# Attention's four projections as 2x2 block products with seven half products, in a hybrid decoder step

## The chip, the cores and the metric

The kernel runs on one core of one Trainium2 chip, as one program in one launch. The metric is the device time in microseconds. Profiles are of one execution each.

## The reference, cut to what matters

```python
D_MODEL, SEQ, DEC_BATCH, PAST_LEN, PAGE_SIZE = 1024, 1024, 8, 1024, 128
B_HEADS, B_DH = 16, 64
def trunk(x, ...):                       # prompt: 1 x 1024 rows; samples: 8 rows with a paged cache
    h, s = hgrn_layer(x, ...)            # first half: gated linear recurrence, 8 heads
    u = rms_norm(h, norm_kv)
    k, v = split(u @ w_kv)               # 1024 x 1024 each
    k = rms_norm(k per head, k_norm)
    logf = log_sigmoid(u @ w_fgate + b_fgate)
    q, gate = split(rms_norm(h, norm_g) @ w_in)    # 1024 x 1024 each
    q = rms_norm(q per head, q_norm)
    # causal for the prompt; for a sample: 1024 cached keys and its own
    p = softmax(q k^T / 8 + c_q - c_k)   # c: cumulative logf, per head
    o = (p @ v) * silu(gate)
    return h + o @ w_o
```

All data is float32. The prompt's 1024 rows and the 8 samples are treated as N = 1032 columns of one matrix `h_t` (features on the partitions).

## The kernel before

The program is written engine by engine with semaphores; each engine runs its own list in the order in which it is written out, and a wait holds up everything behind it on that engine. There are three stages: the recurrence over eight heads (to about 655 us), its output projection with the norm over nine tiles of rows (`tile`, to about 809 us), and the attention, which this change is about.

The attention runs over PAIRS = 8 pairs of heads, `pair(p)` in each engine's list. Each pair has 128 columns of the four projections k, q, v and gate (here g). On TensorE a projection is three pieces of 344 columns by eight blocks of 128 features (`kq`, `values`, `gate_in`), written into banks 0 and 1 in turn; the order of these and of the small products (means of squares for the norms, transposes of k, of v and of the samples) is one list, `ring_order`, and ScalarE empties every one of them (`kq_out`, `v_out`, `g_out`, and so on).

The prompt's attention goes in eight rows of 128 queries: `scores(p, i)` on TensorE, `row_max(p, i)` on VectorE, `soft(p, i)` on ScalarE (exponential, sum, normalised weights), `turn_rows(p, i)` on TensorE (transposes), copies by `turn_a` (ScalarE) and `turn_v` (VectorE), and every second row the product with the values, `weighted(p, m)`. From row 4 on a row fills all four banks of scores, so its `scores` wait for the row before to be turned and copied. Between these steps TensorE does pieces of the projections of this pair (v, g) and of the next (k, q).

The samples' attention over the cache: SyncE loads blocks of 512 KB of cached keys into a ring of four (`k_in`) and of cached values (`v_in`); GpSimd multiplies each block with the queries (`times_q`, line 720); VectorE reduces it (`score`, line 1500); `tops` on VectorE forms the maxima and on GpSimd reduces them over the partitions (line 702), after which come `shift`, `dec_e`, `weigh`, TensorE's `decode`, `smp_sum`, `turn_num` and `smp_out`. Two groups of four samples a pair, both within the pair. The queries of the samples go to memory and come back spread over the partitions (`q_spread`, lines 707 to 710).

The gate: `gate_abs`, `gate_ln`, `gate_in`, `gate_sig` and `gate` for pair p run in pair p + 1. The outputs of all heads stay in `o_t`. VectorE also scales each loaded weight block by the norm's gain (`scale_w`, line 392). At the end `y_part` multiplies all heads' outputs by w_o.

The first half of the kernel already has the scheme that the change brings to the attention. `unit` (line 1694) is one of fourteen units, each of four matmuls of 258 columns, for two projections at once; `unit_copy` (ScalarE) empties two of seven units and `unit_add` (VectorE, line 1149) adds the other five; `w_sums` (GpSimd, lines 627 to 630) forms the sums of weights.

In the trace one float32 matmul of the program is two instructions.

## Time and profile before

| | us |
|---|---|
| time, median of 3 runs (lowest, highest) | 1737.03 (1736.64, 1741.09) |
| the profiled execution | 1736.7 |
| its span, first to last instruction | 1735.0 |
| the recurrence | 0 to 655 |
| output projection and norms | 655 to 809 |
| start of the attention | 809 to 859 |
| pairs 0 to 6 | 859 to 1524, about 95.5 each |
| pair 7 and the output projection | 1524 to 1735 |

The mean granted clock of TensorE is 0.988 of its full rate. A reader of such a profile looks at the busy times of the engines first, then at the same table by stretches, then at what each wait of the busiest engine was for, and last at the other engines in order of time, since an engine's list can be late although its busy share is low.

### The profile page before, as it was taken

The page shows a single profiled execution, that of the slowest core. Times are in us where ns is not written, and L with a number is a line of the kernel's source. Part 1 is how long each engine was busy: PE and PEld are TensorE (multiplying, and loading weights), DVE is VectorE, ACT ScalarE, POOL GpSimd, SP SyncE. Part 2 cuts the span into 40 slices and gives each one's busy share as a digit, 9 for nine tenths or more (in the row PEclk, how much of TensorE's full clock was granted, in tenths as well). Part 3 has the DMA queues.
Part 4 walks back from the last instruction along what each step waited for, and adds up shares of the span by engine and source line. Part 5 has one row for each costly group of instructions (what it writes and reads, how often), then busy time and mean ns, then how long its engine had stood idle before and what let it go on. Part 6 is the DMA issues. An engine that isn't in the chain of part 4 may idle for free.

```text
span 1735.0 us, 23215 instructions
## 1 busy us (share of the span) xinstructions
PE 1666.4 (96%) x8777; PEld 1156.8 (67%) x8777; DVE 966.1 (56%) x1746; ACT 665.4 (38%) x1296; POOL 374.5 (22%) x273
## 2 busy tenths in 40 slices
PE   6999999999999999999999999999999999998998
PEld 4787878888888886443566666666666666665443
DVE  6668695868677775212345546455465655464310
ACT  3324242333323242111345454455454454544100
POOL 5022232222222200100140323222140412232000
PEclk9999999999999999999999999999999999999999
DMA  9480927365463723423324435243525444272121
GB/s 259 143 257 26 267 63 219 96 186 146 135 184 104 233 90 111 129 87 115 90 74 140 164 110 194 99 158 110 171 85 159 134 137 167 86 245 96 49 83 40
DMA packets 252226, 235.94 MB, mean 136 GB/s; under 512 B 22843, under 2 KB 219643, under 8 KB 252115
## 3 DMA queue, kind: packets, MB, share of 16 engines
q1 hardware_dynamic: 241970, 201.04, 37.8%
q0 software_dynamic: 10144, 33.42, 5.7%
q8 instruction: 70, 1.15, 0.3%
q14 instruction: 42, 0.34, 0.1%
HBM read 209.46 MB, written 92.07 MB: 174 GB/s over the span
## 4 chain that ended last, share of the span: by engine, by line
PE 82%; DVE 7%; ACT 4%; issue 4%; DMA 2%; POOL 1%; SPq 0%; DVEq 0%; ACTq 0%; POOLq 0%
PE psum L1694 18%; PE psum L1890 13%; PE psum L1701 7%; PE psum L2106 6%; PE psum L1754 6%; PE psum L1929 5%; PE psum L1954 4%; PE psum L1906 4%; PE psum L1975 3%; PE psum L1961 3%; PE psum L1669 2%; PE psum L1996 2%; PE psum L1898 1%; PE psum L1792 1%; DVE arena L1245 1%
## 5 line engine op out<-in xcount | busy, mean ns | idle before, releaser
L1694 PE MATMUL psum<-arena 128*128 128x258 f32 x1680 | 400.0, 391 | 20.5 <-DVE arena L1149 12.9
L1694 PEld LDWEIGHTS psum<-arena 128*128 128x128 f32 x1680 | 316.3, 194 | 80.6 <-DVE arena L1149 18.7
L1890 PE MATMUL psum<-arena 128*128 128x344 f32 x768 | 236.9, 459 | 1.4 <-DVE arena L1354 0.7
L1890 PEld LDWEIGHTS psum<-arena 128*128 128x128 f32 x768 | 141.9, 191 | 81.6 <-issue 8.4
L720 POOL TENSOR_TENSOR arena<-arena 128x1024 f32<-128x1024 f32 x64 | 160.2, 2532 | 116.6 <-issue 113.2
L976 ACT ACTIVATE arena<-psum,arena 128x256 f32<-128x256 f32 (+7 forms) x128 | 93.6, 737 | 162.1 <-DVE arena L1436 162.1
L1149 DVE TENSOR_TENSOR arena<-arena,psum 128x258 f32<-128x258 f32 x150 | 62.8, 419 | 129.3 <-PE psum L1694 128.8
L1444 DVE COPY arena<-psum 128x128 f32<-128x128 f32 (+3 forms) x64 | 48.4, 756 | 151.6 <-PE psum L1961 151.2
L2106 PE MATMUL psum<-arena 128*128 128x512 f32 (+1 forms) x288 | 127.2, 600 | 2.9 <-DVE arena L1484 2.9
L1701 PE MATMUL psum<-arena 128*128 128x512 f32 (+1 forms) x288 | 128.0, 600 | 0.1
L1929 PE MATMUL psum<-arena 128*128 128x344 f32 x384 | 118.9, 464 | 0.0
L1906 PE MATMUL psum<-arena 128*128 128x344 f32 x384 | 117.9, 457 | 0.0
L1754 PEld LDWEIGHTS psum<-arena 128*128 128x128 f32 x896 | 108.1, 192 | 4.5 <-issue 1.0
L1754 PE MATMUL psum<-arena 128*128 128x64 f32 x896 | 106.1, 271 | 0.0
L2106 PEld LDWEIGHTS psum<-arena 128*128 128x128 f32 (+1 forms) x288 | 51.4, 181 | 73.9 <-issue 70.7
L1929 PEld LDWEIGHTS psum<-arena 128*128 128x128 f32 x384 | 71.9, 192 | 39.9 <-issue 6.8
L1906 PEld LDWEIGHTS psum<-arena 128*128 128x128 f32 x384 | 71.8, 192 | 37.6 <-ACT arena L922 2.0
L1701 PEld LDWEIGHTS psum<-arena 128*128 128x128 f32 (+1 forms) x288 | 51.1, 181 | 68.6 <-issue 68.6
L985 ACT ACTIVATE arena<-arena 128x256 f32<-128x256 f32 (+7 forms) x128 | 92.4, 769 | 2.1
L822 ACT ACTIVATE arena<-arena 128x1024 f32<-128x1024 f32 x56 | 59.2, 1058 | 84.5 <-DVE arena L1188 83.4
L1954 PE MATMUL psum<-arena 64*128 64x512 f32 (+3 forms) x384 | 79.5, 518 | 8.6 <-DVE arena L1444 8.6
L1500 DVE TENSOR_REDUCE arena<-arena 128x16 f32<-128x1024 f32 x64 | 76.4, 1215 | 17.7 <-POOL arena L720 17.4
(246 smaller groups left out, 2364.7 us busy)
## 6 DMA issues: line engine op xcount, KB each, us to landing
k_pages<-in_cache_k SPq DMA_DIRECT2D x64, 512.0 KB, 6.5
v_pages<-in_cache_v SPq DMA_DIRECT2D x64, 512.0 KB, 7.0
arena<-k_pages SPq DMA_DIRECT2D x64, 512.0 KB, 4.0
arena<-v_pages SPq DMA_DIRECT2D x64, 512.0 KB, 5.4
arena<-in_w_in_a SPq DMA_DIRECT2D x32, 512.0 KB, 6.9
arena<-in_x_prompt SPq DMA_DIRECT2D x16, 512.0 KB, 6.2
arena<-in_w_kv SPq DMA_DIRECT2D x16, 512.0 KB, 5.5
arena<-in_w_in_b SPq DMA_DIRECT2D x16, 512.0 KB, 6.3
```

Of the source, the lines that this page charges most:

```text
L720: pool.tensor_tensor(k_ring[:, b], k_ring[:, b], q_all[:, HALF * g + b:HALF * g + b + 1, :].broadcast_to([P, PAGES, P]), ALU.mult).then_in ...
L976: ins = act.activation(weights[:, x, 0:n], rows[:, x, 0:n], ACT.Exp, bias=top[:, at:at + 1], scale=-1.0, accum_out=total[:, at:at + 1])
L985: act.activation(weights[:, x, 0:n], weights[:, x, 0:n], ACT.Copy, scale=inv[:, at:at + 1]).then_inc(p_set, 1)
L1500: dve.tensor_reduce(lg[:, b, :, 0:PAGES].rearrange("p x j -> p j x"), k_ring[:, b].rearrange("p j (x d) -> p j x d", x=2), AX.X, ALU.add). ...
L1694: ins = pe.matmul(bank[n % 2][:, 0:PIECE], w[:, k, :], x[:, k, :], start=(k == 0 and r in (0, 1, 3, 4)), stop=(k == HK - 1), skip_group_ch ...
L1701: ins = pe.matmul(dst[0:rows, :], o_heads[h][:, cols(t)], w_o[:, h, 512 * j:512 * j + 512], start=(h == 0 or lo == AH - 1), stop=(h == AH ...
L1754: ins = pe.matmul(bank[2 + l % 2][:, t * UPPER:(t + 1) * UPPER], f[:, t * P:(t + 1) * P], q, start=True, stop=True)
L1890: ins = pe.matmul(slot[name][:, 0:W3], (w_k, w_q)[y][:, k, :], h_t[:, k, part3(n)], start=(k == 0), stop=(k == KT - 1))
L1906: ins = pe.matmul(slot[f"g{n}"][:, 0:W3], w_g[:, k, :], h_t[:, k, part3(n)], start=(k == 0), stop=(k == KT - 1))
L1929: ins = pe.matmul(slot[f"v{n}"][:, 0:W3], w_v[:, k, :], h_t[:, k, part3(n)], start=(k == 0), stop=(k == KT - 1))
L1954: ins = pe.matmul(dst[:, x, lo:hi], q_t[p % 2][rows, cols(i)], k_t[p % 2][rows, lo:hi], start=True, stop=True)
L2106: ins = pe.matmul(bank[j][0:rows], o_t[:, h, cols(t)], w_ob[h][:, 512 * j:512 * j + 512], start=(h == 0), stop=(h == AH - 1))
```

## The change

The four projections become two pairs of projections (k with q, v with g), each a 2x2 block product: the 1024 features are two halves, the 1032 columns are two halves, and with sums of the inputs (`x_sum`, formed once) and sums of the weights (formed for each pair) seven half products do the work of eight. A pair of projections is fourteen units, each four matmuls of 252 or 264 columns. ScalarE copies two of seven units and VectorE adds the other five.

Around it: `ring_order` becomes `item_order`, since the small products now go through bank 7 alone. The sums of squares for the norms are taken from k_t and q_t in memory (`squares`) and no longer from PSUM. SyncE's ring of cached keys is two blocks, not four. The samples of pair p are decoded in rows that reach into pair p + 1, one reduction to a row. The gate of pair p is done in pair p. Heads' outputs of pairs 0 to 5 are stored to memory (`o_store_b`) and loaded again before the output projection. The input sums overwrite parts of `o_t` and of `h_t`, and the start of the attention is rearranged around them. The first half is as it was, but for its units being 252 and 264 columns.

```diff
-PIECE = HN // 2
+SPLIT = (0, 252, HN)
@@ GpSimd
+            def block_sums(one, two, out, done):
+                me.did(pool.tensor_tensor(out[:, 0], two[:, 0:HK], two[:, HK:KT], ALU.add))
+                me.chain(pool.tensor_tensor(two[:, 0:HK], one[:, 0:HK], two[:, 0:HK], ALU.subtract))
+                me.chain(pool.tensor_tensor(out[:, 1], out[:, 0], one[:, 0:HK], ALU.subtract))
+                pool.tensor_tensor(out[:, 2], one[:, HK:KT], out[:, 1], ALU.subtract).then_inc(done, 1)
+            def sums_of_kq(q):
+                pool.wait_ge(w_k_scaled, q + 1)
+                pool.wait_ge(w_q_scaled, q + 1)
...
             def pair(p):
-                pool.wait_ge(q_loaded, 16 * (p + 1))
-                times_q(p, 0)
-                pool.wait_ge(ring.taken, ring.at("vt1", p))
-                pool.dma_start(v_out[:, :, p, :], v_cur).then_inc(v_stored, 16)
+                m = S * p
+                if p:
+                    times_q(m - 3)
+                if p + 1 < PAIRS:
+                    sums_of_kq(p + 1)
+                k_store(p)
+                q_out(p)
+                if p:
+                    times_q(m - 2, m - 1)
+                q_in(p)
+                if p:
+                    tops(p - 1, 1)
+                v_store(p)
+                times_q(m, m + 1)
+                if p + 1 < PAIRS:
+                    sums_of_vg(p + 1)
+                times_q(m + 2, m + 3)
                 tops(p, 0)
...
+                if 0 < p <= OWN:
+                    o_store_b(p - 1)
+                times_q(m + 4)
@@ VectorE, pair p, from row 0
                 row_max(p, 0)
                 if p:
+                    fin(p - 1, 3)
+                    weigh(p - 1, 0)
+                    score(m - 3)
                 turn_v(p, 0)
+                vg_add(p, 10)
+                if nxt:
+                    scale_w(dve, w_q, gain_b, p + 1, w_q_loaded, w_q_scaled)
                 row_max(p, 1)
+                if p:
+                    smp_sum(p - 1, 0)
+                vg_add(p, 11)
+                vg_add(p, 12)
+                if p:
+                    score(m - 2)
                 turn_v(p, 1)
+                vg_add(p, 13)
+                gate_abs(p)
                 row_max(p, 2)
...
                 row_max(p, 3)
+                kq(3)
+                if p:
+                    shift(p - 1, 1)
+                gate_in(p)
+                kq(4)
                 fin(p, 0)
+                score(m)
                 turn_v(p, 3)
+                kq(5)
                 row_max(p, 4)
...
+                kq(6)
+                silu(p)
+                score(m + 1)
                 if nxt:
                     scale_w(dve, w_v, gain_kv, p + 1, w_v_loaded, w_v_scaled)
+                turn_v(p, 4)
+                kq(8)
                 row_max(p, 5)
...
+                if nxt:
+                    scale_w(dve, w_g, gain_b, p + 1, w_g_loaded, w_g_scaled)
+                kq(11)
+                score(m + 2)
+                turn_v(p, 5)
...
+                turn_v(p, 7)
                 if nxt:
                     norm(p + 1, 0)
+                vg(8)
                 if p + 2 < PAIRS:
                     scale_w(dve, w_k, gain_kv, p + 2, w_k_loaded, w_k_scaled)
                 if nxt:
                     norm(p + 1, 1)
@@ ScalarE, pair p
                 soft(p, 3)
+                if p:
+                    dec_e(p - 1, 1)
+                gate_ln(p)
                 turn_a(p, 3)
+                new_in(p)
                 soft(p, 4)
+                kq(7)
+                gate_sig(p)
                 turn_a(p, 4)
+                kq(9)
                 soft(p, 5)
@@ TensorE, pair p
                 scores(p, 0)
                 if p:
                     weighted(p - 1, 3)
+                vg(p, 9)
+                turn_k(p, 0)
+                if p:
+                    decode(p - 1, 0)
+                turn_rows(p, 0)
+                vg(p, 10)
+                turn_k(p, 1)
+                turn_smp(p)
                 scores(p, 1)
+                vg(p, 11, 12)
...
                 turn_rows(p, 1)
+                vg(p, 13)
                 scores(p, 2)
+                kq_n(0)
+                turn_values(p, 0)
+                kq_n(1)
...
                 scores(p, 3)
+                kq_n(3)
+                weighted(p, 0)
+                kq_n(4)
                 turn_rows(p, 3)
+                new_score(p)
+                kq_n(5)
                 scores(p, 4)
```

## Rows read from the trace of the kernel before

**Rows 1.** The page's first part: busy us, share of the span and instructions of each engine.

```profile
PE 1666.4 (96%) x8777; PEld 1156.8 (67%) x8777; DVE 966.1 (56%) x1746; ACT 665.4 (38%) x1296; POOL 374.5 (22%) x273
```

**Rows 2.** Table by stretches: busy of PE, PEld, DVE, ACT, POOL, then granted clock, DMA.

```profile
1146.00:1241.00 95.00, 93.59 (x559) 60.90 (x557) 51.79 (x116) 49.47 (x111) 25.00 (x16) 1.00 0.43 139
```

**Rows 3.** TensorE's waits in the stretch of one pair, 1146 to 1241.5.

```profile
PE psum L1954 <- DVE arena L1444: 1.0, 1, 1.0
```

**Rows 4.** GpSimd in order of time over one pair: start, duration, instruction, idle before.

```profile
1171.77 1.08 POOL L727 DMA_DIRECT2D out_v_prompt<-arena  x1 [4.17 <-ACT arena L966]
1179.84 0.40 POOL L702 PARTITION_ALL_REDUCE arena<-arena  x1 [6.99 <-issue]
1180.11 0.73 POOL L730 DMA_DIRECT2D out_v_sample<-arena  x1
1187.70 10.29 POOL L720 TENSOR_TENSOR arena<-arena 128x1024 f32<-128x1024 f32 x4 [6.87 <-issue]
1237.07 0.73 POOL L707 DMA_DIRECT2D out_k_sample<-arena  x1 [0.47 <-ACT arena L941]
1237.81 0.52 POOL L708 DMA_DIRECT2D q_rows<-arena  x1
1244.62 0.59 POOL L710 DMA_DIRECT2D arena<-q_rows  x1 [6.29 <-DMA q_rows<-arena]
```

**Rows 5.** The page's groups of instructions: the projections before (busy us, mean ns).

```profile
L1890 PE MATMUL psum<-arena 128*128 128x344 f32 x768 | 236.9, 459 | 1.4 <-DVE arena L1354 0.7
L1929 PE MATMUL psum<-arena 128*128 128x344 f32 x384 | 118.9, 464 | 0.0
L1906 PE MATMUL psum<-arena 128*128 128x344 f32 x384 | 117.9, 457 | 0.0
```

**Rows 6.** The chain that ended last: sixteen instructions of 344, and of 258 columns.

```profile
1164.45 4.84 PE psum L1890 x16
...
72.30 3.54 PE psum L1694 x16
```

**Rows 7.** Groups of VectorE: addition of a unit, reduction of a block, scaling of weights.

```profile
L1149 DVE TENSOR_TENSOR arena<-arena,psum 128x258 f32<-128x258 f32 x150 | 62.8, 419 | 129.3 <-PE psum L1694 128.8
L1500 DVE TENSOR_REDUCE arena<-arena 128x16 f32<-128x1024 f32 x64 | 76.4, 1215 | 17.7 <-POOL arena L720 17.4
L392 DVE TENSOR_TENSOR arena<-arena 128x1024 f32<-128x1024 f32 x32 | 46.3, 1449 | 8.8 <-DMA arena<-in_w_kv 8.6
```

**Rows 8.** GpSimd in order of time: a weight sum while VectorE is quiet.

```profile
38.00 1.27 POOL L629 TENSOR_TENSOR arena<-arena 128x512 f32<-128x512 f32 x1
```

**Rows 9.** Groups of GpSimd: the four weight sums, over the first half.

```profile
L629 POOL TENSOR_TENSOR arena<-arena 128x512 f32<-128x512 f32 x15 | 41.6, 2772 | 1.2
L630 POOL TENSOR_TENSOR arena<-arena 128x512 f32<-128x512 f32 x15 | 38.2, 2549 | 1.2
L628 POOL TENSOR_TENSOR arena<-arena 128x512 f32<-128x512 f32 x15 | 24.9, 1659 | 0.0
L627 POOL TENSOR_TENSOR arena<-arena 128x512 f32<-128x512 f32 x15 | 20.4, 1359 | 159.0 <-PE psum L1694 156.5 <-DMA arena<-in_w_in_a 2.5
```

**Rows 10.** TensorE, then ScalarE, in order of time: row 3, weighted(p, 3), the gate.

```profile
1171.24 1.13 PE L1954 MATMUL psum<-arena 64*128 64x512 f32 x4
1237.76 3.46 PE L1975 MATMUL psum<-arena 128*64 128x256 f32 x32
...
1175.95 1.34 ACT L985 ACTIVATE arena<-arena 128x512 f32<-128x512 f32 x2
1240.87 1.05 ACT L1002 ACTIVATE arena<-arena 128x1032 f32<-128x1032 f32 x1
```

**Rows 11.** TensorE in order of time: a decode in a pair, and after a wait.

```profile
1200.94 1.93 PE L1996 MATMUL psum<-arena 128*2 128x128 f32 x64
...
1580.12 0.39 PE L1991 MATMUL psum<-arena 128*128 128x8 f32 x2 [2.50 <-DVE arena L1522]
1580.44 3.57 PE L1996 MATMUL psum<-arena 128*2 128x128 f32 x64
```

More of the change, by code:

```diff
@@ L744, in _ @@
+            times_q(S * PAIRS - 1)
+            tops(PAIRS - 1, 1)
+            for t in range(2, TT + 1):
                 pool.wait_ge(yb_v, 2 * t + 2)
@@ new lines, in sm_out, with vt_out @@
+            def sm_out(q):
+                act.wait_ge(items.done, items.at("sm", q))
+                if q:
+                    act.wait_ge(ks_stored, 16 * q)
+                    act.wait_ge(q_stored, 16 * q)
+                act.copy(smp_tok[0:S], bank[7][0:S, 0:2 * P]).then_inc(items.taken, 1)
+            def vt_out(p, j):
+                act.wait_ge(items.done, items.at(f"vt{j}", p))
+                if j == 0 and p:
+                    act.wait_ge(pv_done, 4 * p)
+                    act.wait_ge(v_stored, 16 * p)
+                act.copy(v_cur[:, 4 * j:4 * j + 4, :], bank[7]).then_inc(items.taken, 1)
@@ new lines, in new_in @@
+            def new_in(p):
+                act.wait_ge(items.done, items.at("sn", p))
+                if p:
+                    act.wait_ge(df_set, 2 * p)
+                for g in range(2):
+                    lg = lgt[g].rearrange("p (b x j) -> p b x j", x=2, j=9)
+                    ins = act.activation(lg[:, :, :, PAGES], bank[7][:, 8 * g:8 * g + 8].rearrange("p (b x) -> p b x", x=2), ACT.Copy,
+                                         scale=-float(P))
+                ins.then_inc(items.taken, 1)
@@ L1894, in means, with open_item @@
[L1894 to L1908 removed]
+            def open_item(name, p):
+                n = items.next(name, p)
+                if n > 1:
+                    pe.wait_ge(items.taken, n - 1)
+                return bank[7]
@@ new lines, in b_unit @@
+            def b_unit(n, one, two, w_sum, scaled, summed, u):
+                if u == 0:
+                    for s in scaled:
+                        pe.wait_ge(*s)
+                elif u == 1:
+                    pe.wait_ge(*summed)
+                if n in (1, 4, 8, 11):
+                    pe.wait_ge(h_sums, {1: 3, 4: 7, 8: 7, 11: 8}[n])
+                if n >= 2:
+                    pe.wait_ge(*b_units.taken(n - 2))
+                product(n, one[:, 0:HK], one[:, HK:KT], two[:, 0:HK], two[:, HK:KT], w_sum, u).then_inc(b_units.done, 1)
@@ new lines, in kq, with vg, means @@
+            def kq(q, *us):
+                for u in us:
+                    b_unit(kq_b(q, u), w_k, w_q, sums_kq, ((w_k_scaled, q + 1), (w_q_scaled, q + 1)), (kq_sums, q + 1), u)
+            def vg(p, *us):
+                for u in us:
+                    b_unit(vg_b(p, u), w_v, w_g, sums_vgb, ((w_v_scaled, p + 1), (w_g_scaled, p + 1)), (vgb_sums, p + 1), u)
+            def means(q, y, *ns):
+                for n in ns:
+                    dst = open_item(f"m{'kq'[y]}{n}", q)
+                    pe.wait_ge(sq_done, 2 * q + y + 1)
+                    pe.matmul(dst[:, 0:W3], bones, sq[y][:, part3(n)], start=True, stop=True, skip_group_check=True).then_inc(items.done, 1)
```

1091 lines of the change are left out of this document (572 added, 519 removed).

## The prediction

> **What bounds the kernel now.** I read the page's engine table first: TensorE is busy for 1666.4 us of a 1735.0 us span and GpSimd for 374.5 us [rows 1]. A reader should ask next whether TensorE's work is really end to end, so the second view is the table by stretches. The attention repeats every 95.5 us, once for each of eight pairs of heads. In one such stretch of 95 us TensorE is busy for 93.6 us, VectorE for 51.8, ScalarE for 49.5 and GpSimd's recorded instructions for 25.0 [rows 2]. Its only wait of note in a pair is that of the first scores, 1.0 us, for a VectorE copy [rows 3]. So today the attention is bound by TensorE, and an operation less on it is time won as long as the other engines keep ahead. The third view, GpSimd in order of time, shows that its busy share is misleading: around each of the two partition reductions of a pair it does nothing on record for 6.9 to 7.0 us, once before it and once after it, marked "issue", though no operand is late [rows 4]. Four such gaps a pair are 28 us, so GpSimd is really taken for 25 + 28 = 53 of 95 us.
>
> **What is removed.** The four projections of a pair are 192 instructions of 344 columns, 1536 in all [rows 5]. Sixteen of them take 4.84 us in the chain, and 0.19 us of that is the tail of the group, so one costs 0.289 us; sixteen of 258 columns, the form that the first half of the kernel already uses, take 3.54 us, 0.2165 us each with the tail out [rows 6]. A pair goes from 192 x 0.289 = 55.5 us to 28 units x 8 x 0.2165 = 48.5 us. That is 7.0 us a pair and 56 us in all, the most the change can give. TensorE's own work for a pair becomes 93.6 - 7.0 = 86.6 us; the walk below, operation by operation, comes to 86.
>
> **What is added.** VectorE gets 20 additions from PSUM a pair at 0.42 us [rows 7], 8.4 us, and loses about 0.5 us of gating, so about 60 of 87 us. ScalarE loses some 3 us. GpSimd gets two sets of four weight sums. Their cost has two ends: 1.27 us each when nothing else reads, 5.1 us a set [rows 8], and the means 1.36, 1.66, 2.77 and 2.55 us of the first half, 8.3 us a set [rows 9]. I take 6 us, near the lower end, because in the attention VectorE mostly reads PSUM while they run, and keep both ends. GpSimd then has 53 + 12 (10 to 17) us, and about 8 us more of waiting for the trip of the queries through memory, since it now waits for it explicitly: 73 us of a pair. It fits on paper. What decides is order, since VectorE takes its work strictly in turn and several items in its list wait for GpSimd.
>
> **The order, walked through for one middle pair.** Times are from the pair's first scores; durations are those of the rows, and copies and maxima that have no row of their own are taken as in the same operation before. VectorE scales w_q after row 0, at 12.3 (TensorE's part before it is the 3.4 us product of row 7, two units, the 2.0 us decode [rows 10, 11] and short transposes). GpSimd can only then form the k/q sums (to 18.3). It next issues the stores of keys and queries (2.4 us, two of their rows in [rows 4]) and then multiplies cached block m-2, 2.5 us, to 23.2. But VectorE has the reduction of that block, 1.2 us [rows 7], ahead of turning row 1, which TensorE has ready at 16.4. So turn_v(1) ends at 24.8 instead of 16.8, the last value unit is added at 25.2, and unit kq 1, which needs its bank, waits on TensorE from 21.7 to 25.3. Row 2's maximum is queued behind too, and the first head's weights come about 3.5 us after that maximum begins (in row 3, a size larger, they come 4.3 us after the end of the scores, at 1176.6 for scores that end at 1172.3 [rows 10]). Scores of row 3 end at 35.9 instead of 28.0: loss 7.9 us.
>
> Second, in row 3 VectorE must run the gate's second step before turn_v(3), and that step waits for two ScalarE passes of 1.05 us [rows 10] which sit behind row 3's softmax: ready at 44.2, then an addition, a copy and the reduction of block m. GpSimd has m only at 47.2 (18.3, stores 2.4, two multiplications 5, waiting for the queries' store and fetching them 1.9, a gap of 7.2, the reduction 0.9, stores of values 1.8, a gap of 7.2, a multiplication 2.5). TensorE ran out of work at 42.9 and gets row 3 back at 49.2: loss 6.3, of which 4.0 would be there without GpSimd.
>
> Third, in row 4 VectorE's silu waits for ScalarE's sigmoid, which waits for the copy of unit kq 7, and turn_v(4) is behind silu (1.2), a reduction (1.2) and a weight scaling of 1.2 to 2.5 us (1.45 on average [rows 7]). TensorE has only row 4's transposes and one unit meanwhile: loss 3.9 with a small wait before the decode. Fourth, row 5 has the reduction of block m+2 ahead of turn_v(5), and GpSimd makes the v/g sums, which wait for w_g scaled in that same row, ahead of that block: 6 + 2.5 us after the scaling. Loss 5.5. Fifth, at the pair's end the norm of q, which the next pair's first scores need, is queued on VectorE behind the addition of unit vg 8 (that waits for a ScalarE copy) and a scaling of w_k; with row 7 that is 3.9 us. Small waits make 0.3.
>
> Sum: 7.9 + 6.3 + 3.9 + 5.5 + 3.9 + 0.3 = 27.8 us of waiting over about 86 us of work, a pair of 113.8 us against 95.5: 18.3 us more. Every step from turn_v to turn_v is a loop through all engines, so none of it is made up in the next pair.
>
> **The clock.** After TensorE idled 2.50 us late in the kernel, the 64 instructions of a decode took 3.57 us where they take 1.93 us in a pair without such a wait [rows 11]. That is the step between the levels 2.4 and 1.2 GHz. With five or six idle stretches of 2 to 6 us a pair, some of whose slow work lies where TensorE waits anyway, I add 4 us a pair (0 to 9, from 1.6 us times none or all of them). The granted clock should fall from 1.00 in a pair to about 0.9.
>
> **The ends.** The stretch between the first half and the pairs takes over 23 units (39.8 us against 27.8 of projections) and eight input subtractions of about 1.2 us on VectorE, half of them under earlier tiles: 8 us later at pair 0. Pair 0 has no block of a pair before it in rows 1 and 2: 4.5 us longer than now. The last pair has five units instead of 48 instructions of each projection it had (19 us less work), but the same waits in rows 2 to 6 with GpSimd's gaps: 6 us less in all. The extra stores and loads of the heads' outputs (about half a megabyte each) run on queues that wait for little; I cost them at nothing beyond GpSimd's issue time, as the product that needs them comes one pair later; if that cover were gone, some 5 us once.
>
> Sum against the profiled execution, 1736.7 us (1.7 of it outside the span, and 0.3 below the median of the runs): 1736.7 + 8 + 4.5 + 6 x 18.3 - 6 + 7 x 4 = 1881, so **1880 us**.
>
> **A rule beside the rows.** The gaps of [rows 4] have no instruction in the trace. The Trainium skill's GPSIMD Engine Reference, Instruction dispatch, says that the first call of a freshly loaded kernel pays a load of approximately 6 us with no visible instruction. The trace agrees in kind, with 6.9 to 7.0 us. By 6 us in place of 7.2 the chain to row 3 would be 2.4 us shorter, of which 2.2 count before VectorE's own order binds, 13 us in all: 1868. The same page, Key points, says that GpSimd contends with VectorE instructions with two SBUF inputs; it speaks against the change, as the third rival does from rows.
>
> **Rivals.**
> *Everything is hidden and TensorE stays the bound.* For it: 93.6 of 95 us busy, and the same units with the same sums run in the first half with few waits. Against it: there, no reduction of a block waits behind the sums, and no reduction gap either. It would give 7.0 a pair back, less a little: 1736.7 - 56 + 5 = 1685. It is the case with the other sign; it decides if turn_v(1), (3) and (5) are done before TensorE has finished the unit after them. Chance 0.12.
> *GpSimd is early, but the order on VectorE and ScalarE holds.* Then row 1 loses nothing, row 3 loses 4.0, row 4 3.9, row 5 0, the end 3.9, a pair is about 98.6 + 2 for the clock: 5.1 x 6, and 8, 2 and -7 at the ends, 1770. It needs the sums and gaps to be half of what the rows show, or the scaled weights some 10 us earlier. Chance 0.2.
> *The upper prices.* Sums of 8.3 us twice, gaps of 8.2 us and all the slow clock: 4.6 + 2 + 5 more a pair, 1881 + 6 x 11.6 = 1950. Chance 0.08.
> Forecast 0.58. The change not doing what it says (a projection left whole) has 0.02; the instruction counts would show it, and the time would be near the old.
>
> **From cases to numbers.** The range goes from 1765, to take in the second rival, to 1935: the forecast's own is 1830 to 1930 (clock 0 to 9 a pair). That leaves out 0.12 + 0.02 below and about half of the upper prices. Faster by over 0.3% 0.12, within 0.3% 0.02, slower by more 0.86; 0.3% is about what a measurement of this kernel can tell from no change.
>
> **What would show it.** Right: a pair of 108 to 124 us; GpSimd or a reduction of a cached block named as what VectorE waited for before turn_v(1), (3), (5); 20 to 30 us of idle TensorE a pair; four gaps of about 7 us a pair still there; a lower granted clock. Wrong: TensorE over 97% busy in a pair of 88 us (first rival), or VectorE reductions that never wait for GpSimd with a pair near 100 us (second). The forecast fails first if the sums take under 4 us or if VectorE reaches the scaling of w_q much earlier than 12 us into the pair.

## The result and the profile after

The changed kernel takes 1921.42 us (median of 4 runs, 1920.36 to 1924.78) against 1739.06 us (1736.64 to 1741.81) for the kernel before on the same chip: a ratio of 1.105, 95% interval 1.103 to 1.108. The forecast was 1880 us, with a range of 1765 to 1935. The profiled execution spans 1918.7 us, 183.7 more than before.

First the page's engine table of the changed kernel, to hold against [rows 1], and then its table by stretches for pair 3, to hold against [rows 2] (busy time of PE, PEld, DVE, ACT, POOL, granted clock, DMA share, GB/s).

```profile
PE 1698.4 (89%) x9033; PEld 1241.1 (65%) x9033; DVE 1024.4 (53%) x1911; ACT 646.2 (34%) x1248; POOL 454.2 (24%) x343
```

```profile
1222.00:1344.50 122.50, 100.52 (x593) 72.49 (x593) 58.87 (x137) 47.59 (x104) 35.47 (x25) 0.89 0.33 112
```

The change takes matmul columns away, and yet TensorE is busy for longer, 100.5 us of a pair for 93.6. The clock in the same row says why it isn't more work: 0.89 for 1.00. And 22.0 us of the pair are idle where there was 1.4. These are TensorE's four largest kinds of wait in that pair (total, times, longest), where [rows 3] had one of 1.0 us:

```profile
PE psum L2126 <- DVE arena L1576: 11.9, 3, 4.4
PE psum L2126 <- DVE arena L1534: 3.0, 1, 3.0
PE psum L2133 <- ACT arena L1068: 2.8, 2, 2.3
PE psum L1861 <- DVE arena L1230: 2.2, 1, 2.2
```

L2126 are the scores and L1576 is turn_v, the copy of the turned weights out of PSUM: the scores of rows 4, 5 and 6 wait for it. The others are the next pair's first scores behind the norm of q (L1534), `turn_rows` (L2133) behind ScalarE's weights, and unit kq 1 (L1861) behind the addition that frees its bank (L1230). VectorE's own waits in that pair tell what held the copy back. L1636 is the reduction of a cached block (`score`), L1604 is silu, L1600 the gate's second step:

```profile
DVE arena L1636 <- POOL arena L790: 12.1, 2, 7.0
...
DVE arena L1604 <- ACT arena L1084: 5.4, 1, 5.4
...
DVE arena L1600 <- ACT arena L1080: 4.3, 1, 4.3
```

GpSimd in order of time in that pair (start, duration, idle before) answers to [rows 4]:

```profile
1235.80 1.27 POOL L658 TENSOR_TENSOR arena<-arena 128x512 f32<-128x512 f32 x1 [23.87 <-issue]
...
1239.73 1.28 POOL L661 TENSOR_TENSOR arena<-arena 128x512 f32<-128x512 f32 x1
1240.95 1.08 POOL L774 DMA_DIRECT2D out_k_prompt<-arena  x1
...
1243.14 4.67 POOL L790 TENSOR_TENSOR arena<-arena 128x1024 f32<-128x1024 f32 x2
...
1255.80 0.39 POOL L757 PARTITION_ALL_REDUCE arena<-arena  x1 [6.81 <-issue]
...
1265.92 5.65 POOL L790 TENSOR_TENSOR arena<-arena 128x1024 f32<-128x1024 f32 x2 [8.19 <-issue]
```

The reader sees the first loss whole: weight sums, stores, and only at 1243.14 the product of block m-2. The 23.87 us of "issue" ahead of the sums are a wait too: they begin as soon as VectorE has scaled w_q (L418, first line below), and the second set, at 1298.84, as soon as it has scaled w_g (last line). So GpSimd's lateness itself comes out of VectorE's list. On VectorE the reduction of m-2 stands ahead of turn_v(1):

```profile
1234.45 1.22 DVE L418 TENSOR_TENSOR arena<-arena 128x1024 f32<-128x1024 f32 x1
...
1245.55 1.22 DVE L1636 TENSOR_REDUCE arena<-arena 128x16 f32<-128x1024 f32 x1 [5.13 <-POOL arena L790]
1246.68 0.41 DVE L1576 COPY arena<-psum 128x256 f32<-128x256 f32 x1
...
1267.07 2.29 DVE L1600 SCALAR_TENSOR_TENSOR arena<-arena 128x1032 f32<-128x1032 f32 x1 [4.27 <-ACT arena L1080]
...
1269.95 1.21 DVE L1636 TENSOR_REDUCE arena<-arena 128x16 f32<-128x1024 f32 x1
1271.07 0.68 DVE L1576 COPY arena<-psum 128x512 f32<-128x512 f32 x1
...
1297.48 1.22 DVE L418 TENSOR_TENSOR arena<-arena 128x1024 f32<-128x1024 f32 x1
```

Last, what follows the idle stretches on TensorE in the same pair:

```profile
1290.07 2.57 PE L2126 MATMUL psum<-arena 64*128 64x512 f32 x8 [3.25 <-DVE arena L1576]
...
1308.59 3.36 PE L2126 MATMUL psum<-arena 64*128 64x512 f32 x8 [4.38 <-DVE arena L1576]
1311.88 3.81 PE L2149 MATMUL psum<-arena 128*64 128x256 f32 x24
```

The first scores of the pairs start at 871.30, 979.12, 1100.09, 1221.93, 1344.45, 1465.35, 1587.10 and 1708.46. So of the 183.7 us, 11.9 arise before pair 0 (which began at 859.45), 16.3 in pair 0, 156.3 in pairs 1 to 6 (26.1 each, a pair being 121.6 for 95.5), and 0.8 come back at the end.

### The profile page after: what moved, and what is told of

It is laid out like the page before. It is cut to its first block and busy times, and to the rows that moved or that the text cites. A ratio compares the mean times of both kernels' runs of the same rounds, so it can differ in the third digit from the quotient of the medians.

```text
span 1918.7 us, 24200 instructions
## 1 busy us (share of the span) xinstructions
PE 1698.4 (89%) x9033; PEld 1241.1 (65%) x9033; DVE 1024.4 (53%) x1911; ACT 646.2 (34%) x1248; POOL 454.2 (24%) x343
## 5 line engine op out<-in xcount | busy, mean ns | idle before, releaser
L1861 PE MATMUL psum<-arena 128*128 128x252 f32 (+1 forms) x3472 | 854.3, 398 | 36.5 <-DVE arena L1230 28.2
L1861 PEld LDWEIGHTS psum<-arena 128*128 128x128 f32 x3472 | 666.8, 198 | 182.9 <-issue 53.1
L1230 DVE TENSOR_TENSOR arena<-arena,psum 128x252 f32<-128x252 f32 (+1 forms) x310 | 129.8, 419 | 269.3 <-PE psum L1861 254.7
L2126 PE MATMUL psum<-arena 64*128 64x512 f32 (+3 forms) x384 | 108.3, 681 | 114.4 <-DVE arena L1576 95.0
L790 POOL TENSOR_TENSOR arena<-arena 128x1024 f32<-128x1024 f32 x64 | 153.8, 2419 | 148.5 <-issue 97.0
L658 POOL TENSOR_TENSOR arena<-arena 128x512 f32<-128x512 f32 x31 | 40.4, 1305 | 540.2 <-issue 336.4
L1059 ACT ACTIVATE arena<-psum,arena 128x256 f32<-128x256 f32 (+7 forms) x128 | 93.6, 737 | 220.8 <-DVE arena L1568 220.8
L2126 PEld LDWEIGHTS psum<-arena 64*128 64x128 f32 x384 | 44.3, 243 | 162.6 <-issue 138.9
L868 ACT COPY arena<-psum 128x252 f32<-128x252 f32 (+1 forms) x124 | 45.8, 369 | 299.1 <-PE psum L1861 299.1
L1636 DVE TENSOR_REDUCE arena<-arena 128x16 f32<-128x1024 f32 x64 | 77.8, 1216 | 93.3 <-POOL arena L790 93.0
L1938 PEld LDWEIGHTS psum<-arena 128*128 128x128 f32 x896 | 108.2, 192 | 4.4 <-issue 1.0
L2133 PE MATMUL psum<-arena 128*128 128x128 f32 x576 | 81.1, 281 | 22.8 <-ACT arena L1068 22.4
L2133 PEld LDWEIGHTS psum<-arena 128*128 128x128 f32 x576 | 63.9, 142 | 45.7 <-ACT arena L1068 39.6
L2149 PE MATMUL psum<-arena 128*64 128x256 f32 (+1 forms) x640 | 88.2, 434 | 0.0
L1576 DVE COPY arena<-psum 128x128 f32<-128x128 f32 (+3 forms) x64 | 48.1, 752 | 64.3 <-PE psum L2133 64.2
```

Source lines behind the costliest of these rows:

```text
L790: pool.tensor_tensor(k_ring[:, m % 2], k_ring[:, m % 2], q_all[:, m % S:m % S + 1, :].broadcast_to([P, PAGES, P]), ALU.mult).then_inc(kq_m ...
L1059: ins = act.activation(weights[:, x, 0:n], rows[:, x, 0:n], ACT.Exp, bias=top[:, at:at + 1], scale=-1.0, accum_out=total[:, at:at + 1])
L1230: dve.tensor_tensor(out, more, bank[n % 2][:, 0:size(u)], ALU.add).then_inc(of.by_dve, 1)
L1636: dve.tensor_reduce(lg[:, b, :, 0:PAGES].rearrange("p x j -> p j x"), k_ring[:, m % 2].rearrange("p j (x d) -> p j x d", x=2), AX.X, ALU.a ...
L1861: ins = pe.matmul(bank[n % 2][:, 0:size(u)], w[:, k, :], x[:, k, :], start=(k == 0 and r in (0, 1, 3, 4)), stop=(k == HK - 1), skip_group_ ...
L1938: ins = pe.matmul(bank[2 + l % 2][:, t * UPPER:(t + 1) * UPPER], f[:, t * P:(t + 1) * P], q, start=True, stop=True)
```

## Experiments

**First set: each of the four causes alone.** Four kernels, each one edit of the changed kernel. The first moves every reduction of a cached block behind the turn_v that it stood ahead of (row 1 shown, rows 2 to 5 alike):

```diff
@@ VectorE, pair p
-                if p:
-                    score(m - 2)
                 turn_v(p, 1)
                 vg_add(p, 13)
                 gate_abs(p)
                 row_max(p, 2)
+                if p:
+                    score(m - 2)
```

> Only VectorE's list is changed: in rows 1 to 5 the reduction of a cached block stands behind the row's turn_v, not ahead of it. Theory (order: TensorE waits because turn_v(1) and turn_v(5) are queued behind blocks that GpSimd has late): TensorE no longer waits 2.2 + 2.3 us in row 2 and 4.4 us ahead of the scores of row 6, but shift(p-1,1) in row 3 then waits for GpSimd's partition reduction for some 4 us. A pair goes from 121.6 to about 108 us, the time from 1921 to about 1830 (ratio to before 1.05). Rival (the cost is the gaps and the work of GpSimd itself, which stays): no change, a pair of 120 us. Rival (the cost is the unit scheme and the slow clock): no change either.

Measured: 1856.61 us, ratio 1.067 (1.065 to 1.069), 65 us less than the changed kernel; a middle pair 112.6 us, pair 0 94.0. The direction is the theory's, the size isn't (about 1830 and 108 us): with the blocks out of the way gate_abs came to lie beside GpSimd's products and took 5.60 us for 0.91, and TensorE waited 4.74 us ahead of turn_rows(2). The kernel with all edits of order, below, shows the same in its rows.

The second moves the next pair's norm of q, with its new score, ahead of the last unit and the scaling of w_k:

```diff
-                vg(8)
-                if p + 2 < PAIRS:
-                    scale_w(dve, w_k, gain_kv, p + 2, w_k_loaded, w_k_scaled)
                 if nxt:
                     norm(p + 1, 1)
                     new_score(p + 1)
+                vg(8)
+                if p + 2 < PAIRS:
+                    scale_w(dve, w_k, gain_kv, p + 2, w_k_loaded, w_k_scaled)
```

> Only the end of a pair on VectorE is changed: the norm of the next queries and new_score stand ahead of the addition of unit 8 and of the scaling of w_k. Theory (order): the 2.9 us that TensorE waits before the first scores of each pair goes, 3 us in each of seven pairs, 21 us, ratio to before about 1.093. Rival (ScalarE's norm steps are what is late): no change.

Measured: 1887.83 us, ratio 1.084 (1.082 to 1.087), 34 us less, with no wait left ahead of the first scores. That is more than the 21 us expected: the product behind these scores, weighted(p - 1, 3), takes 3.46 us for 5.02, so the slower work behind the wait went with it.

The third leaves out the maximum over the partitions, and so GpSimd's four gaps a pair; the decode then subtracts another value:

```diff
-                pool.partition_all_reduce(m_all[g], top8[g], P, bass.bass_isa.ReduceOp.max).then_inc(top_all, 1)
+                pool.tensor_copy(m_all[g], top8[g]).then_inc(top_all, 1)
```

> The maximum over the partitions in the samples' softmax is left out: GpSimd copies the partition's own maxima. With it all four code loads of a pair go, some 28 us of GpSimd's time. Theory (order): GpSimd has block m ready about 1 us before VectorE asks for it, and waits for VectorE at both weight sums, so the gaps are not on the path: a pair within 1.5 us of 121.6, ratio to before 1.09 to 1.105. Rival (GpSimd's gaps are the cost): up to 14 us a pair less, 90 us in all, ratio 1.05.

Measured: 1897.04 us, ratio 1.090 (1.088 to 1.093), 24 us less, just inside the theory's range of ratios. A middle pair is 118.7 us for 121.6, 2.8 less where the theory had at most 1.5, though some 28 us of gaps left GpSimd in it; another 8.1 us came back in the last part. VectorE still waits 12.0 us a pair for the products of blocks m-2 and m+2, which stand behind the weight sums.

The fourth moves the gate's second step from ahead of kq 4 to behind row_max(4), and silu from ahead of turn_v(4) to behind row_max(5):

```diff
-                gate_in(p)
                 kq(4)
...
                 row_max(p, 4)
+                gate_in(p)
...
-                silu(p)
...
                 row_max(p, 5)
+                silu(p)
                 gate_first(p)
```

> Only the gate's places on VectorE are changed: gate_in goes from ahead of turn_v(3) to behind the maximum of row 4, silu from ahead of turn_v(4) to behind the maximum of row 5. Theory (order): the waits of 4.3 and 3.3 us ahead of the scores of rows 4 and 5 shrink to about 0 to 1, block m then being what row 3 waits for, about 6 us a pair and 1 to 2 more by the clock, 50 us in all, ratio to before about 1.075. Rival (GpSimd late in row 3): row 3 gains nothing and the whole less than 25 us.

Measured: 1879.96 us, ratio 1.081 (1.079 to 1.083), 41 us less, for the 50 expected. VectorE's waits for GpSimd in a pair rose from 12.1 to 16.4 us at once: with the gate out of the way, block m is what holds row 3. There the rival was right, since TensorE's wait ahead of the scores of row 4 went only from 4.25 to 3.93 us; the gain is row 4's own, where the wait of 3.25 us ahead of the scores of row 5 is gone.

**Is it the weight sums or GpSimd's other lateness?** Here three of four operations of each set are left out in pairs 1 to 7 (so q, k, v and the gate come out as other values):

```diff
+            def last_sum(one, two, out, done):
+                pool.tensor_tensor(out[:, 2], one[:, HK:KT], out[:, 1], ALU.subtract).then_inc(done, 1)
...
-                block_sums(w_k, w_q, sums_kq, kq_sums)
+                (block_sums if q == 0 else last_sum)(w_k, w_q, sums_kq, kq_sums)
```

> Left out: the first three of the four operations of each set of weight sums of attention's pairs 1 to 7 on GpSimd (the last one stays, so the stages keep their signals; the outputs are not the reference's). That takes 3.8 of 5.1 us a set off GpSimd, twice a pair. Theory (the sums stand ahead of the decode blocks on GpSimd, and VectorE takes each block ahead of a turn_v): block m-2 is ready 3.8 us sooner in row 1 and block m+2 sooner by up to 7.0 us, the wait that VectorE had for it, of which 3.8 go: 7.6 us a pair at most, and TensorE's time after the waits shortens with its clock: 50 to 70 us in all, 1850 to 1872 us, ratio 1.065 to 1.077. Rival (GpSimd's lateness is that of its waits for VectorE and DMA, or VectorE's own queue binds right behind): under 20 us, 1901 to 1920, ratio above 1.094.

Measured: 1849.90 us, ratio 1.064 (1.062 to 1.066), 72 us less for 3.8 us off each set. VectorE still waits for GpSimd, and for the gate as before:

```profile
DVE arena L1639 <- POOL arena L793: 6.7, 3, 3.1
DVE arena L1607 <- ACT arena L1087: 5.4, 1, 5.4
```

So the sums are a cause of their own. A set stands before a block that stands before a turn_v, and 7.6 us of GpSimd's time became about 11 of the pair (110.4 for 121.6 on average). In pair 3, 110.1 us for 122.5, TensorE idles for 16.1 us instead of 22.0 and is busy for 93.9 instead of 100.5, so about half of the gain is the clock. The wait ahead of the scores of row 6 fell from 4.38 to 0.48 us, while that ahead of row 4, which is the gate's, grew from 4.25 to 5.64.

**Is the slow work after a wait really the wait's doing?** Two kernels add work to TensorE where it idles, ahead of the scores of rows 4, 5 and 6: multiplications of the identity by itself, 24, 18 and 24 of them in the first.

```diff
+                def fill(u, count):
+                    n = kq_b(p + 1, u)
+                    if nxt:
+                        pe.wait_ge(*b_units.taken(n - 2))
+                        for _ in range(count):
+                            pe.matmul(bank[n % 2][:, 0:128], ident, ident, start=True, stop=True, skip_group_check=True)
...
                 last((1, 0, 3))
+                fill(6, 24)
...
                 last((1, 3, 5))
+                fill(9, 18)
...
-                kq_n(12, 13)
+                kq_n(12)
+                fill(13, 24)
+                kq_n(13)
```

> The changed kernel with work added: 24, 18 and 24 matmuls of 128x128 with the identity, whose output nobody reads, on TensorE where it idles ahead of the scores of rows 4, 5 and 6 of every pair but the last. At the full clock one is about 0.13 us (0.130 for a transpose of that size), so 3.1, 2.3 and 3.1 us in idle stretches of 4.25, 3.25 and 4.38 us; nothing that TensorE waits for moves. Theory (idle stretches cost their length and then again at the lower clock that is granted after them; 8.6 us of a pair were put down to that): the scores of rows 4 to 6 come back to their full-clock 2.0 to 2.3 us from 2.5 to 3.4, weighted(2) to 2.6 from 3.8, the granted clock rises from 0.943 to 0.96 or more, and the kernel is faster by 2 to 6 us a pair: 1880 to 1907 us, ratio 1.081 to 1.096, though it does 8.5 us more TensorE work a pair. Rival (what looks like clock is contention or waiting, and added work costs what it overhangs): 1921 to 1945 us, ratio 1.105 to 1.118, the scores' durations as they were.

Measured: 1911.15 us, ratio 1.100 (1.098 to 1.103), clock 0.969. Each multiplication took 0.234 us, not 0.13, so they overhung the waits; it was 10 us faster all the same, between the theory's range and the rival's. What the expectation calls output that nobody reads isn't quite that: units kq 6, 9 and 13 add to what an earlier unit left in that bank, which the added work replaces, so these keys and queries are other values. The second kernel has counts that fit:

```diff
-                            pe.matmul(bank[n % 2][:, 0:128], ident, ident, start=True, stop=True, skip_group_check=True)
+                            pe.matmul(bank[n % 2][:, 384:512], ident, ident, start=True, stop=True, skip_group_check=True)
...
-                fill(6, 24)
+                fill(6, 18)
...
-                fill(9, 18)
+                fill(9, 12)
...
-                fill(13, 24)
+                fill(13, 18)
```

> The changed kernel with added matmuls again, 18, 12 and 18 of them at the same three places, now into columns of the bank that nothing else uses. One took 0.234 us in the run before (24 in 5.62 us), not 0.13, so there they overhung the idle stretches by 1.4, 0.9 and 1.1 us; now they take 4.2, 2.8 and 4.2 us in 4.25, 3.25 and 4.38. Theory (idle time costs the clock of what follows): the pair comes from 118.2 us to about 115, the kernel to 1880 to 1895 us, ratio 1.081 to 1.090, 26 to 41 us faster than without the added work. Rival (the gain of 10 us in the run before came from something else, such as the spoilt data): 1905 to 1921 us, ratio 1.096 or more.

Measured: 1893.16 us, ratio 1.089 (1.086 to 1.092), 28 us faster than without the added work, inside the theory's range. TensorE in order of time around rows 5 and 6, and the stretch of pair 3:

```profile
1277.42 2.84 PE L2198 MATMUL psum<-arena 128*128 128x128 f32 x24
1280.83 1.56 PE L2126 MATMUL psum<-arena 64*128 64x512 f32 x8 [0.57 <-DVE arena L1576]
...
1291.38 4.18 PE L2198 MATMUL psum<-arena 128*128 128x128 f32 x36
...
1297.75 1.78 PE L2126 MATMUL psum<-arena 64*128 64x512 f32 x8 [0.40 <-DVE arena L1576]
1299.45 2.60 PE L2149 MATMUL psum<-arena 128*64 128x256 f32 x24
```

```profile
1211.50:1331.00 119.50, 106.43 (x689) 81.70 (x691) 58.64 (x138) 47.60 (x104) 35.66 (x25) 0.94 0.35 115
```

The scores take 1.56 and 1.78 us for 2.57 and 3.36, the weighted sum 2.60 for 3.81. Of the 106.4 us busy 12.9 are added work (5.91 + 2.84 + 4.18), which leaves 93.5 for what took 100.5: 7 us of a pair were the clock after these three waits alone. The pair itself is only 3.1 us shorter (119.4 for 122.5; over pairs 1 to 6 117.8 for 121.6), because the added work and the idle time left, 12.9 and 13.1, are more than the 22.0 before. Both kernels with added work form other keys and queries; that these other values make the time isn't excluded by them alone, but the orders below bring the clock back with all values right.

**Do the orders' gains add?** All edits of order together, and the scaling of w_v behind turn_v(4):

```diff
+                turn_v(p, 4)
+                kq(8)
                 if nxt:
                     scale_w(dve, w_v, gain_kv, p + 1, w_v_loaded, w_v_scaled)
-                turn_v(p, 4)
-                kq(8)
```

> All order edits at once: score() behind turn_v in rows 1 to 5, gate_in and silu behind the row maxima of rows 4 and 5, the next pair's norm ahead of vg(8) and scale_w(w_k), and scale_w(w_v) behind turn_v(4) and kq(8). Theory (each loss is a place of its own on one path through TensorE and VectorE): the gains of the three kernels run before add, 64.8 + 33.6 + 41.5 = 140 us, for 1782 us, ratio about 1.025, a middle pair of 101 to 103 us and less than 6 us of TensorE's idle time in a pair. Rival (the losses overlap: behind each of them the next one is already late, above all GpSimd's sums and maxima): the gains don't add, and it comes out at 1815 to 1850 us, ratio 1.045 to 1.065, with a wait for GpSimd (VectorE's weigh or shift behind the reduction, or the units behind the weight sums) as the largest that is left.

Measured: 1828.93 us, ratio 1.053 (1.051 to 1.055): the rival. The gains add to 140 us and gave 92.5. A pair is 108.9 us on average, and the new waits are on VectorE operations that themselves became long. VectorE in order of time, rows 1 and 5 of pair 3 (L1596 is gate_abs, L1676 and L1678 are smp_out):

```profile
1198.12 5.60 DVE L1596 TENSOR_SCALAR arena<-arena 128x1032 int32<-128x1032 int32 x1
...
1248.97 1.03 DVE L1676 TENSOR_TENSOR arena<-arena 64x4 f32<-64x4 f32 x1
...
1250.22 1.12 DVE L1678 TENSOR_TENSOR arena<-arena 64x4 f32<-64x4 f32 x1
1251.37 2.27 DVE L1676 TENSOR_TENSOR arena<-arena 64x4 f32<-64x4 f32 x1
...
1253.87 2.06 DVE L1678 TENSOR_TENSOR arena<-arena 64x4 f32<-64x4 f32 x1
```

In the changed kernel gate_abs took 0.91 us, with the end of a product beside it, and the small ones 0.15. gate_abs has GpSimd's two block products beside it (1198.49 to 1203.16), the small ones the weight sums up to 1251.3 and two products to 1255.92. They hold up row 2's maximum, and `dec_fin`, on which weighted(2) waits 4.08 us.

**Second and third set of orders.** The second takes these operations out of GpSimd's way and weigh out from behind the gate:

```diff
-                gate_abs(p)
                 row_max(p, 2)
...
                 turn_v(p, 2)
                 if p:
+                    score(m - 2)
                     score(m - 1)
                     tops(p - 1, 1)
+                gate_abs(p)
                 row_max(p, 3)
...
-                gate_in(p)
                 if p:
                     weigh(p - 1, 1)
                 fin(p, 1)
+                gate_in(p)
...
                 gate_first(p)
+                if p:
+                    smp_out(p - 1, 1)
                 kq(10)
```

> On top of all order edits: gate_abs and score(m-2) behind turn_v(2), weigh(1) and fin(1) ahead of gate_in, smp_out(p-1,1) from behind kq(12) to ahead of kq(10). With all order edits alone, TensorE still idled in pair 2 for 4.73 us ahead of turn_rows(2), where gate_abs took 5.60 us beside GpSimd's weight sums and product (0.91 us in the changed kernel), 2.08 us ahead of decode and 4.08 us ahead of weighted(2), where four operations of smp_out, 64x4 elements each, took 6.48 us beside GpSimd's products (0.63 us in the pair's other call). Theory (VectorE operations that lie beside GpSimd's are stretched, and what is left of the pair's excess over TensorE's own 86 us is these three waits and the clock after them): 9 to 14 us a pair come back in six pairs and some in the others, for 1735 to 1775 us, ratio 0.998 to 1.021, a middle pair of 95 to 100 us. Rival (the stretched operations are only moved to beside other GpSimd work, or a wait for GpSimd's products or maxima stands right behind): under 30 us, 1799 to 1829 us, ratio 1.035 or more.

Measured: 1783.99 us, ratio 1.026 (1.024 to 1.028), 45 us less; the theory's direction, but short of its range, with a middle pair of 102.1 us for the 95 to 100 expected. Gate_abs, now with no GpSimd work beside it, takes 0.69 us and the four operations that had been long 0.15 and 0.16; but one of the pair's other call, moved beside the product of block m-2, now takes 3.28. The part of the rival that came true: a wait for GpSimd stood right behind. VectorE and TensorE in pair 3:

```profile
1203.05 1.22 DVE L1636 TENSOR_REDUCE arena<-arena 128x16 f32<-128x1024 f32 x1 [5.94 <-POOL arena L790]
```

```profile
1207.14 0.57 PE L2164 MATMUL psum<-arena 128*128 128x8 f32 x2 [5.55 <-DVE arena L1658]
1207.64 3.60 PE L2169 MATMUL psum<-arena 128*2 128x128 f32 x64
```

Two kernels start from here. One leaves the partition maximum out again, as the third kernel above did:

> The second set of orders with the maximum over the partitions left out (a plain copy in its place, so the decode's shift is another; outputs with it). In the changed kernel that gained 24 us, 2.4 us of a pair, though four gaps of about 7 us go in a pair. Theory (there the gaps lay beside waits for the gate and the norm; with the second orders product m waits for the second gap of 7.0 us and VectorE waits 5.94 us for product m, and 5.19 us for m+4 behind the other reduction's 7.84 us gap): now the gaps are on the path, and leaving them out gives 5.5 + 2.3 + 1.5 us a pair, 55 to 70 us, for 1714 to 1729 us, ratio 0.986 to 0.995. Rival (the products wait for their loads or for TensorE's units, not for the code load, so the gap merely fills that wait): under 25 us, 1760 to 1784 us, ratio 1.012 or more.

Measured: 1717.20 us, ratio 0.987 (0.985 to 0.990), 67 us less, inside the theory's range, where the same edit gave 24 us in the changed kernel: the gaps were there all along, but behind other waits. The other keeps the maximum and moves the reductions that wait for it:

```diff
                 turn_v(p, 3)
                 kq(5)
-                score(m)
                 row_max(p, 4)
...
                 gate_in(p)
+                score(m)
                 kq(6)
...
-                score(m + 4)
                 vg(6)
...
                     new_score(p + 1)
+                score(m + 4)
                 vg(8)
```

> On top of the second set of orders: score(m) from behind turn_v(3) and kq(5) to behind gate_in, scale_w(w_v) and score(m+1) behind row_max(5), score(m+4) behind the next pair's norm. With the second orders, in pair 3, TensorE idled 5.55 us ahead of decode (VectorE waited 5.94 us for GpSimd's product m with row_max(4) and weigh queued behind), 1.29 us ahead of turn_rows(5) and 1.49 us ahead of the next pair's scores(0) (VectorE waited 5.19 us for product m+4); decode and the unit behind it took 3.60 and 2.67 us for 1.93 and 2.05. Theory (each order that lets VectorE wait for GpSimd ahead of TensorE's next wait costs that wait and the clock after it): 5.5 + 2.3 + 1.3 + 1.5 = 10.6 us a pair in six pairs and part of it in the two others, for 1705 to 1725 us, ratio 0.981 to 0.993, with a middle pair of 91 to 93 us: faster than the kernel before. Rival (the products' readings, later now, make the next loads and products late, and the wait comes back one row on): 1745 to 1784 us, ratio 1.004 or more.

Measured: 1731.18 us (median of 6) against 1739.17, ratio 0.995 (0.993 to 0.997). This version computes all that the reference does and is faster than both kernels: 190 us faster than the changed kernel by the order of VectorE's list alone, and 8 us, half a per cent, faster than the kernel before. Of the 56 us that the prediction gives as the most, that is little: the start of the attention costs 16.1 us more than before, pairs 1 to 6 give back 0.5 each, pair 0 6.4 and the last part 9.2. Its pair 3, then that of the kernel without the maximum:

```profile
1150.00:1244.50 94.50, 89.18 (x591) 66.57 (x591) 63.88 (x137) 47.60 (x104) 35.42 (x25) 1.00 0.43 146
```

```profile
1144.50:1237.00 92.50, 88.50 (x591) 66.42 (x591) 61.58 (x136) 47.75 (x104) 34.17 (x25) 1.00 0.43 149
```

It missed the theory's range by 6 us: a pair came down by 7 us, not 10.6, because the norm now lies beside GpSimd's product and takes 4.04 us for its two operations (2.5 otherwise), and the last pair kept waits of 1 to 3 us.

## Why the prediction was right, and where it wasn't

The time lies in the range, and the waits stand where the walk put them. The 1921 us are nearer to 1880 than the terms of the sum deserve, though, since its three terms for a pair are off in opposite directions.

**TensorE's own work.** Forecast 86 to 86.6 us a pair, 7.0 saved. At the full clock and nearly without waits (the kernel without the maximum, second orders) a whole pair, from first scores to first scores, has 88.8 us of work, and the same stretch of the kernel before 94.1, so 5.3 were saved. The price of a unit was too low: 0.2165 us an instruction doesn't follow from its row, where 3.54 less 0.19, over 16, is 0.209. The difference of two groups gives it: twenty-four instructions of 258 columns take 5.32 us in the chain of the kernel before, sixteen 3.54, so a unit is 1.78 and 28 are 49.8 us for 55.5, 5.7 saved. In the changed kernel three units of 264 columns take 5.61 us and two 3.83, 1.78 again.

**The sums.** Forecast 6 us a set, between 5.1 and 8.3. They measured 1.27 us each, 5.1 a set, the lower end, as [rows 8]. VectorE was mostly waiting while they ran. The gaps of [rows 4] stayed four a pair, 6.8 and 8.2 us around one reduction.

**Row 1.** The dates are right to half a microsecond. From the pair's first scores, block m-2's reduction ended at 24.8 and turn_v(1) at 25.2 (forecast: the product ready at 23.2, turn_v(1) done at 24.8), and unit kq 1 went at 25.6 for 25.3. The loss isn't: TensorE waited 2.19 us for that bank and 2.30 for row 2's weights, and its work between was slower (a unit of 3.57 us for 1.95), so the scores of row 3 end at 38.3 us, where the walk had 35.9.

**Row 3.** Scores of row 4 at 50.0 us for 49.2, but not for the reason that the step gave. The gate's step began only at 45.1 and took 2.29 us beside GpSimd's product, and the block was ready just then: the reduction waited for nothing. TensorE's wait was 4.25 us, where the forecast had 6.3, of which 4.0 without GpSimd. Gate and block are each enough for most of it: 3.93 us with the gate moved, and 3.20 without the maximum, when the block is ready earlier. With the blocks moved and the gate left it is 2.08.

**Rows 4, 5 and the end.** The causes were as named: silu waiting for the sigmoid (5.39 us on VectorE), block m+2 behind the v/g sums (7.01 us), and the norm of q behind vg 8 and w_k (2.93 us on TensorE). All idle time of the pair is 22.0 us where the walk had 27.8; most of the difference lies in rows 1 to 3, partly because slower work filled what would have been waiting.

**The clock** is the term of the sum that was mis-sized. Forecast 4 us a pair from a range of 0 to 9; the pair has 100.5 us of busy time for 88.8 at full clock, so 11.7, outside even that range. The step that failed is "some of whose slow work lies where TensorE waits anyway": the slow work follows each wait directly, and what follows are scores and units on which all else depends. Filling three waits gave back 7 us of it. The two durations of a decode in [rows 11], 1.93 and 3.57 us, were the price, 1.64 us. It was multiplied by too few places, and it was too low for the long waits: six idle stretches of over 2 us would make 9.8, and behind the one of 4.38 us alone scores and weighted sum took 7.2 us for 4.4.

A pair is thus 22.0 + 88.8 + 11.7 = 122.5 us, forecast 27.8 + 86 + 4 = 117.8. The waits were over by 5.8, the work under by 2.8 and the clock under by 7.7; that the sum is off by only 4.7 is in part luck.

**The ends.** Pair 0 begins 11.9 us later, forecast 8: the stretch from 770 to its start has 12 us more of TensorE work, as the forecast's own 39.8 less 27.8 would have it; the 8 took part of that as hidden. Pair 0 cost 16.3 more, forecast 4.5, or 8.5 with the clock. It is waiting: TensorE is busy for 90.2 us of it, 90.1 before, and idles for 17.6 instead of 1.4, and with all edits of order it takes 86.7 us. The last part gave back 0.8 where 6 was forecast (the seven times 4 us of clock cover seven of the eight pairs): its work fell by 12.4 us, not 19, and its idle time grew by 11.6. With the third orders it takes 201.8 us for 211.0.

**The rivals.** "GpSimd is early but the orders hold", 1770, is refuted by the waits. But GpSimd's lateness alone isn't the cause either: moving only what waits for it left 1857. "The upper prices", 1950, had the sums too dear; only its slow clock came true, and its 9 us a pair were still too few. "Everything is hidden", 1685, needs what the third orders do, and even then the pair is 95.0 and not 88 us. The change moves more than the units (the decode into the next pair, the gate, a shorter ring of cached keys, stores of the outputs); no run separates these.

**Two rules beside the rows.** For the gaps, the Trainium skill's GPSIMD Engine Reference, Instruction dispatch, gives approximately 6 us for a load. In pairs 0 to 6 of the changed kernel the traces show 6.7 to 8.9 us where the profile names no VectorE operation as the releaser, once on the way to the reduction and once on the way back. Its Key points say that GpSimd contends with VectorE instructions in a 2-port performance mode or with two SBUF inputs. The trace agrees for two inputs: gate_in went from 1.22 to 2.29 us and a 64x4 multiplication from 0.15 to 3.28. Gate_abs, with one input, went from 0.69 to 5.60; no run here shows in which mode it ran.

## What to carry to other kernels

On an engine that takes its work strictly in turn, put nothing that waits for a slow helper ahead of the operation that the bound engine waits for next; here the same instructions in another order were worth 190 of 1921 us. A change that takes work off the bound engine moves all dates, so walk the order of the other engines through again: this one lost 182 us in one order of VectorE's list and won 8 in another. And price an idle stretch at its length plus the slower work behind it: here 22 us of waits a pair cost 34.

## What the runs showed of the hardware that was not expected

- Added work on an idle TensorE made a kernel faster: 12.9 us of useless multiplications a pair, 28 us less in all, and the granted clock of the stretch from 0.89 to 0.94.
- A VectorE operation beside a GpSimd product can take eight to over twenty times its time: 5.60 us for 0.69 (1032 integer columns, one input), 3.28 us for 0.15 (four columns, two inputs). GpSimd can lose as well: a pair of products took 5.65 us for 4.67 with gate_in in between. It seems that VectorE waits until GpSimd's instruction or pair of instructions is over: gate_abs ran from 1198.12 to 1203.72 beside products that ended at 1203.16, and the last small one to 1255.93 beside products that ended at 1255.92. The length goes with the place: gate_abs took 0.69 us again where the second orders put it, with no GpSimd work beside it. Which of the two engines waits for what, and why, was read from the traces alone; no run isolates it.
- A matmul that starts a new sum in columns 384 to 511 of a PSUM bank seems to alter what later matmuls in columns 0 to 263 of that bank add to: in the second kernel with added work the keys came out changed by about as much as in the first, where columns 0 to 127 had been overwritten. How far this reaches (which columns, which orders) wasn't tried.
